# Inverse RMS roots at three of four places: ScalarE Sqrt, reciprocal and one Newton step in place of an integer seed and three Newton steps

## The reference

```python
def rmsnorm(x, g):
    xf = x.astype(jnp.float32)
    y = xf * lax.rsqrt(jnp.mean(xf * xf, axis=-1, keepdims=True) + EPS)
    return (y * g.astype(jnp.float32)).astype(x.dtype)
...
h = modulate(rmsnorm(x, norm_mix_g[l]), sh_m, sc_m)
z = jnp.einsum('bsd,de->bse', h, w_in[l])
...
y_a = spatial_gating(jax.nn.gelu(z_sgu), v_norm_g[l], sgu_w[l], sgu_b[l])
...
x = x + g_m[:, None, :] * jnp.einsum('bsd,de->bse', merged, w_out[l])
hf = modulate(rmsnorm(x, norm_ffn_g[l]), sh_f, sc_f)
x = x + g_f[:, None, :] * grouped_moe(hf, router_w, router_bias, ...)
return rmsnorm(x, final_norm_g)
```

## Time and profile before

| | us |
|---|---|
| median of 3 runs | 811.03 |
| lowest, highest | 810.52, 811.32 |
| span of the profiled execution | 808.6 |
| TensorE busy in it | 740.2 |
| VectorE busy in it | 600.2 |
| ScalarE busy in it | 383.4 |
| GpSimd busy in it | 196.5 |

### The profile page before, as it was taken

The page is one execution under the profiler, slowest core; times in us unless marked ns, Lnnn a source line. Parts: engine busy times, 40 slices in busy tenths (PEclk is TensorE's granted clock), DMA queues, the critical chain, the costliest instruction groups (busy, mean ns, idle before and its releaser), DMA issues. The chain is left out here.

```text
span 808.6 us, 10644 instructions
## 1 busy us (share of the span) xinstructions
PE 740.2 (92%) x3359; PEld 604.0 (75%) x3360; DVE 600.2 (74%) x823; ACT 383.4 (47%) x339; POOL 196.5 (24%) x74
## 2 busy tenths in 40 slices
PE   2589999999999999999999379999999999999982
PEld 2468888866888888887788368888888888888861
DVE  3772334766476666658556789999999999999976
ACT  5533523342323141324133266777777777777613
POOL 1000000400100000000052111445555554444552
PEclk9799999999999999999997589999999999999997
DMA  8797330431356473917472627599999999999652
GB/s 314 258 364 238 104 130 6 151 104 53 106 173 191 159 255 102 313 52 260 159 251 85 199 104 288 214 372 393 369 356 361 361 360 376 366 393 367 248 221 104
DMA packets 105075, 187.66 MB, mean 232 GB/s; under 512 B 6927, under 2 KB 49999, under 8 KB 104540
## 3 DMA queue, kind: packets, MB, share of 16 engines
q1 hardware_dynamic: 98652, 177.77, 61.8%
q0 software_dynamic: 4784, 7.95, 2.7%
q10 hardware_dynamic: 1616, 1.65, 0.6%
HBM read 180.47 MB, written 16.25 MB: 243 GB/s over the span
## 5 line engine op out<-in xcount | busy, mean ns | idle before, releaser
L747 DVE TENSOR_TENSOR wsplit<-raw,wsplit 128x2048 fp32r<-128x2048 f32 x132 | 299.3, 2288 | 78.9 <-ACT wsplit L521 53.8
L684 ACT ACTIVATE wsplit<-raw 128x2048 fp32r<-128x2048 f32 x96 | 183.9, 1918 | 74.3 <-PE ps L1323 74.3
L469 POOL DMA_INDIRECT expert_rows<-work,dest_now x15 | 108.1, 7209 | 114.3 <-DVE work L1227 114.3
L1321 PE MATMUL ps<-wsplit,hgT 128*128 128x512 f32 x272 | 110.1, 405 | 5.0 <-DVE hgT L1146 5.0
L1323 PE MATMUL ps<-wsplit,hgT 128*128 128x512 f32 x272 | 107.6, 395 | 0.0
L1322 PE MATMUL ps<-wsplit,hgT 128*128 128x512 f32 x272 | 106.8, 392 | 0.0
L1321 PE MATMUL ps<-hT,wsplit 128*128 128x512 f32 x256 | 102.5, 400 | 1.0 <-DVE mx L900 1.0
L1322 PE MATMUL ps<-hT,wsplit 128*128 128x512 f32 x256 | 101.1, 395 | 0.0
L1323 PE MATMUL ps<-hT,wsplit 128*128 128x512 f32 x256 | 101.1, 395 | 0.0
L799 DVE SCALAR_TENSOR_TENSOR raw<-raw,c_silu 128x256 f32 (+1 forms) x128 | 62.0, 484 | 17.1 <-DMA raw<-in_w_ada 13.1
L1321 PEld LDWEIGHTS ps<-wsplit,hgT 128*128 128x128 f32 x272 | 51.9, 191 | 15.6 <-DVE hgT L1146 5.7
(11 more groups left out here) (241 smaller groups left out, 1207.7 us busy)
## 6 DMA issues: line engine op xcount, KB each, us to landing
raw<-in_w_exp_gate SPq DMA_DIRECT2D x32, 1024.0 KB
raw<-in_w_exp_up SPq DMA_DIRECT2D x32, 1024.0 KB
raw<-in_w_exp_down SPq DMA_DIRECT2D x32, 1024.0 KB
raw<-in_w_ada SPq DMA_DIRECT2D x24, 1024.0 KB
raw<-in_w_in SPq DMA_DIRECT2D x20, 1024.0 KB
expert_rows<-tmp SPq DMA_DIRECT2D x4, 1024.0 KB, 12.4
raw<-in_w_branch_a SPq DMA_DIRECT2D x4, 1024.0 KB
raw<-in_w_branch_b SPq DMA_DIRECT2D x4, 1024.0 KB
```

The costliest lines, as they stand in the source:

```text
L469: g.indirect_dma_start(out=y_dram, out_offset=bass.IndirectOffsetOnAxis(ap=dest_now[:, 0:1], axis=0), in_=y, in_offset=None, bounds_check= ...
L684: A_(wsplit[:, c, 0, :], raw[:, c, :], ACT.Copy).then_inc(hi_ready, 1)
L747: V.tensor_tensor(wsplit[:, n, 1, :], raw[:, slot, :], wsplit[:, n, 0, :].bitcast(F32), ALU.subtract).then_inc(lo_ready, 1)
L1321: nc.tensor.matmul(out, w_hi, m_hi_, start=first, stop=False)
```

## The change

Three of the four inverse roots are computed in another way: those of the first norm, of the FFN norm and of the last norm. The one of the spatial gate (`inv_rms(20, NT)`) stays. ScalarE takes the square root of mean + EPS with its Sqrt function, from the sums in `stats`, right behind the squares; VectorE takes the reciprocal z, and makes one Newton step, z (1.5 - 0.5 m z z). For that EPS must lie in a tile (`eps_col`, one more memset on GpSimd), and the function table with Sqrt must be loaded on ScalarE. `root_table` does a Sqrt of one column ahead of each of the three places, so that the load stands there: behind the Silu at the start, behind the last high part of `merged`, and behind the last tile's hidden rows in the tail. Each brings one ACT_TABLE_LOAD that wasn't there. The loads for Gelu, Sigmoid, Exp and Silu stay as many as they were.

```diff
@@ gpsimd @@
             g.memset(base[:, :], 0.0)
+            g.memset(eps_col[:, :], EPS)
@@ scalar @@
+            def square_root(col, n):
+                A_(root[:, 0:n], stats[:, col:col + n], ACT.Sqrt, bias=eps_col[:, 0:1],
+                   scale=1.0 / D).then_inc(rooted, 1)
+
+            def root_table(use):
+
+                A_(root[:, NT + use:NT + use + 1], eps_col[:, :], ACT.Sqrt)
+
             act.wait_ge(cols_ready, 1)
             A_(c_silu[:, :], cols[:, 0:ND], ACT.Silu).then_inc(c_ready, 1)
+            act.wait_ge(consts, 1)
+            root_table(0)
...
+            act.wait_ge(squares, NT)
+            square_root(0, NT)
             act.wait_ge(rms_ready, 1)
...
                 A_(hT[:, 0, k, :], merged[:, k, :], ACT.Copy).then_inc(m_hi, 1)
+            root_table(1)
             for n in range(O0 + 1, O0 + 4):
...
                 A_(hf[:, t, :], x_tiles[:, t, :], ACT.Square, accum_out=stats[:, 24 + t:25 + t]).then_inc(sq2, 1)
+                act.wait_ge(sq2, t + 1)
+                A_(root[:, t:t + 1], stats[:, 24 + t:25 + t], ACT.Sqrt, bias=eps_col[:, 0:1],
+                   scale=1.0 / D).then_inc(rooted, 1)
...
             a_hi(tiles - 1)
 
+            root_table(2)
             act.wait_ge(y_ready, tiles - 1)
...
+            act.wait_ge(fin_sq, NT)
+            square_root(28, NT)
             act.wait_ge(fin_rms_ready, 1)
@@ vector @@
-            def inv_rms_1(col):
...
+            def root_inverse(col, n, count):
+
+                m, half, z = stats[:, col:col + n], nrm[:, 0:n], nrm[:, NT:NT + n]
+                step(V.tensor_scalar(half, m, -0.5 / D, -0.5 * EPS, ALU.mult, ALU.add))
+                dve.wait_ge(rooted, count)
+                step(V.reciprocal(z, root[:, 0:n]))
                 done()
+                step(V.tensor_tensor(m, z, z, ALU.mult))
                 done()
+                step(V.tensor_tensor(m, m, half, ALU.mult))
+                done()
+                step(V.scalar_tensor_tensor(out=m, in0=m, scalar=1.5, in1=z, op0=ALU.add, op1=ALU.mult))
+                done()
+
+            def root_inverse_1(t):
+
+
+                m, half, z, q = stats[:, 24 + t:25 + t], nrm[:, 0:1], nrm[:, NT:NT + 1], nrm[:, 2 * NT:2 * NT + 1]
+                step(V.tensor_scalar(half, m, -0.5 / D, -0.5 * EPS, ALU.mult, ALU.add))
+                dve.wait_ge(rooted, 2 + t)
+                step(V.reciprocal(z, root[:, t:t + 1]))
+                done()
+                step(V.scalar_tensor_tensor(out=q, in0=z, scalar=half, in1=z, op0=ALU.mult, op1=ALU.mult))
+                done()
+                step(V.scalar_tensor_tensor(out=m, in0=q, scalar=1.5, in1=z, op0=ALU.add, op1=ALU.mult))
+                done()
...
-            inv_rms(0, NT)
+            root_inverse(0, NT, 1)
...
-                inv_rms_1(24 + t)
+                root_inverse_1(t)
...
-            inv_rms(28, NT)
+            root_inverse(28, NT, NT + 2)
```

More of the change, by code:

```diff
@@ L91, in tokens_moe_kernel @@
         fin_rms = sb("fin_rms", [P, 1])
+        eps_col = sb("eps_col", [P, 1])
+        root = sb("root", [P, NT + 3])
         inv_count = sb("inv_count", [P, 16])
@@ L162, in tokens_moe_kernel @@
         h_aff, h_hi, h_lo = map(sem, ("h_aff", "h_hi", "h_lo"))
-        chain = sem("chain")
+        chain, rooted = sem("chain"), sem("rooted")
         v_gelu, v_centred, v_square, v_ready, u_ready = map(
@@ L772, in inv_rms @@
                     done()
-            def inv_rms_1(col):
[L777 to L782, removed]
+            def root_inverse(col, n, count):
[3 more added lines that the diff above has]
+                step(V.reciprocal(z, root[:, 0:n]))
                 done()
-                step(V.tensor_scalar(zi, powers[2].bitcast(I32), -0.5,
-                                     float(0x5F3759DF - (2 << 23) - (1 << 31)), ALU.mult, ALU.add))
+                step(V.tensor_tensor(m, z, z, ALU.mult))
                 done()
[L788 to L794, removed]
+                step(V.tensor_tensor(m, m, half, ALU.mult))
[12 more added lines that the diff above has]
+                done()
             def ada(acc, slot, a):
```

## The result

| | before | after |
|---|---|---|
| median, beside each other (us) | 811.17 (4 runs) | 802.27 (4 runs) |
| lowest, highest (us) | 810.52, 813.09 | 800.20, 803.69 |
| ratio | | 0.9887, 95% interval 0.9871 to 0.9902 |
| span of the profiled execution (us) | 808.6 | 801.9 |

The change gains 8.9 us, where 3.3 were forecast. The two profiled executions are 6.7 us apart and not 8.9, since they are the fastest of the four before and the slowest of the four after.

The account below looks back on a forecast made before the run. TensorE was taken to bound the body, and the chain through the norm the front and tail. Start 1.15, FFN norm 1.0 and tail 1.18 sum to 3.3 us off 811.0, giving 807.7; range 806.3 to 810.0.

Parts of the forecast that it names:

- Inside the body a faster VectorE is worth nothing beyond such a wait: In the TensorE-bound body, faster VectorE work gains only what TensorE spends waiting, 0.7 us on GpSimd's add in the FFN norm.
- Between 60 and 480 us it waits only around the router: Reading of TensorE's waits: only around the router, with 0.7 us on GpSimd and 0.2 us on ScalarE in the FFN norm.
- Start, 1.15 with bounds 0.8 and 1.25: First norm: from last read of the squares to first modulation operation 1.43 us in place of 2.58, a gain of 1.15.
- that wait as a sign of being wrong: At the start: the prediction is wrong if VectorE waits for w_ada at 13.6 us.
- FFN norm, 1.0 with ends 0.68 and 1.36: TensorE's 0.68 us wait for the third tile's hf goes; saves 1.36 if the clock's fall keeps its time; 1.0 taken.
- Everything behind hangs on this chain and shifts with it: Behind the FFN norm: router, gather and expert tiles all start earlier along with it.
- Tail, 1.18: Last norm: from last read of the squares to first scaling 1.53 us in place of 2.71, a gain of 1.18.
- Table loads: nothing: The three added table loads, at the start, before the out-projection's splits and in the tail, cost nothing, hidden by idle time.
- The rival by the Trainium skill: Each table load stalls ScalarE another 1.28 to 1.38 us, at start and tail; 808.3 to 809.2, take 808.8; chance 0.12.
- only the tail counts: Start's gain meets late w_ada or TensorE's restart, 0.68 becomes a wait for ScalarE; 1.2 us left, 809.8; chance 0.16.
- the clock takes it back: The clock's fall in the FFN norm comes sooner, costing up to 7.0 us, 814.7 with the whole price; chance 0.05.
- the third sign of being wrong: Whole kernel: the prediction is wrong if the stretches at 1.2 GHz are longer in sum.

Follow-up runs that it names:

- e1_pad64: The kernel before with one unused tile of 64 bytes in front of hT, nothing else changed; 807.02 us beside 812.54, ratio 0.993.
- e2_tiles_last: The changed kernel with its two new tiles declared behind `work`, so that hT keeps its old address; 810.66 us, ratio 0.9988.
- e11_both_pads: The kernel before with 64 unused bytes ahead of `raw` and 64 ahead of hT; 808.14 us in one run, beside 812.98.

## Why the prediction was wrong

- **What was missed.** The step is the sentence "Inside the body a faster VectorE is worth nothing beyond such a wait", and with it the assumption that TensorE's 740 us of work stay what they are. True of VectorE, but the sum then had no term for the body at all. The new tiles moved one operand of the wide matmuls by 64 bytes against the other, and that gave 5.5 us (e1_pad64). By stage it is 93.85 - 91.76 = 2.1, 2.75 and 1.2 us in A, B and C, together 6.1. None of the rivals held it, and no range built from the roots' terms could have. The evidence was at hand, though not its price: the kernel declares two new tiles ahead of hT, and its profile before has two means for what is the same matmul, 390 ns where both operands lie in wsplit and 395 to 400 where hT is streamed.
- **Direction.** That the kernel came out faster, clear of the noise, is owed to the 64 bytes, and is luck as far as the forecast goes: at the old addresses the roots gave 1.0 us with an interval that holds zero.
- **A reading.** "Between 60 and 480 us it waits only around the router" is not what the view says. It also has three waits of TensorE for VectorE, of 1.0, 1.0 and 0.9 us; the last, at the product with w_out, is where the start's gain went.
- **Start, 1.15 with bounds 0.8 and 1.25.** Right to its step: 0.30 for the root as taken, 1.63 in place of 2.58 gives 0.95, with a wait for w_ada of 0.31 us, where the bound left 0 to 0.3. The prediction had named that wait as a sign of being wrong; it cost 0.2 us against the forecast and is not what failed. What failed is that it was carried to the end. In e2_tiles_last 0.48 is left behind the restart near 61 us, and at w_out, where a transfer comes no earlier, nothing.
- **FFN norm, 1.0 with ends 0.68 and 1.36.** In e2_tiles_last 0.05 became 0.88 at the third tile and 1.14 behind the router, 1.1 in all; over all kernels 0.85. Right in cause and near in size, though the 0.68 us to be saved is one value of a wait that ran from nothing to 1.1 us in the kernels with the old root. "Everything behind hangs on this chain and shifts with it" failed: the gather gave back 0.85 of it, and the loop the rest.
- **Tail, 1.18.** 1.35 measured in after. The two handoffs around the root are 0.03 and 0.03 us, where 0.14 and 0.10 were taken for them: the root started at 792.48, 0.03 behind the read's end, and the reciprocal at 792.81 behind the root's end at 792.78.
- **Table loads: nothing.** Right. The rival by the Trainium skill, "ScalarE: Activation LUTs", What ACT_TABLE_LOAD costs, would have a further 1.38 us of drain at each load. The dummy roots start 0.02, 0.01 and 0.02 us behind the ends of the loads that start at 4.78, 376.66 and 770.63 us, and the loads themselves 0.02 us or less behind the activations ahead of them, so the measurement decides against it here.
- **Rival "only the tail counts", 1.2 us gained.** For the roots by themselves this came nearest: 1.3 us of span in e2_tiles_last, and 1.0 (-0.2 to 2.2) as time. Its reasons were others, a late w_ada or a restart; it was w_out and the gather. At the old addresses the interval holds the rival's 1.2 and neither the forecast's 3.3 nor its lower bound of 2.5. At the new ones the two estimates, 2.4 and 3.5 us, are too wide to decide between them.
- **Rival "the clock takes it back".** In part, and not because of the roots. The mean granted clock is 0.955 in after for 0.962 in before, the third sign of being wrong that the prediction gave; but it is 0.954 in e1_pad64, which has no new root. The fall in the FFN norm came 7.0 us behind the end of the wide matmuls before. In after it is in this stretch:

```profile
428.50:429.00 0.50, 0.50 (x6) 0.50 (x6) 0.50 (x1) 0.00 (x0) 0.00 (x0) 0.79 0.51 205
```

A mean of 0.79 puts the fall near 428.8, 5.6 us behind the transposes' start at 423.17, and the third tile's transposes then took 1.61 us for 1.10 in the earlier trace rows. That goes with an FFN stage 0.7 us shorter in after and not 1.1. But in the kernel with the new root at the start alone, which has the old FFN norm, it also fell early, 5.4 us behind, while in e2_tiles_last, with the new one, it was 6.9. The price there is 15.50 - 15.14 = 0.36 us between after and e2_tiles_last, and never the 7.0 of the rival. A second one stands in the tail: in after the clock is at one half from 783.8 to 787.2 us, and the last 20 wide matmuls take 6.42 us, behind a longer wait for ScalarE. Before and then after:

```profile
789.15 5.13 PE L1607 MATMUL ps<-wsplit,tail_sel 128*128 128x512 f32 x20 [2.65 <-ACT wsplit L717]
```

```profile
783.58 6.42 PE L1634 MATMUL ps<-wsplit,tail_sel 128*128 128x512 f32 x20 [3.64 <-ACT wsplit L737]
```

By these two, after's lead over before falls from 6.5 us at the end of the expert loop to 797.80 - 792.45 = 5.35 at the last read of the squares. The longer matmuls do not come from the roots: e11_both_pads, with no new root, has them (6.59), and e2_tiles_last, with all of them, has not (5.12). The wait is taken up in the last section.

## What to carry to other kernels

A change that declares or drops a tile moves everything that is placed behind it. Before a few microseconds are put down to new instructions, compare the time from one start to the next of the same wide matmuls in a stage that the change doesn't touch, and run the old kernel with an unused tile of the same size: it takes one line. Where TensorE is the bound, try the distance between streamed and held operand for itself; here one spare tile of 64 bytes was worth more than three rewritten normalizations. And a gain at the start counts only up to the first transfer whose landing doesn't move with it.

## What was not expected of the hardware

- Wide matmuls (128x512, fp32r) at 2.4 GHz took 227, 229 or 233 ns from start to start in the three long stages, by the distance of their two operands in on-chip memory modulo 256 bytes: 0, 64, and the others tried (32, 128, 192, 224). Shifting both together changed nothing. The first 70 or so, at a distance of 64, took 233.3 in one kernel and 229.1 in another with the same addresses.
- A GpSimd tensor_tensor on large tiles held up a VectorE operation of one element. Before, GpSimd and then VectorE:

```profile
408.32 9.41 POOL L477 TENSOR_TENSOR wsplit<-raw,wsplit 128x2048 fp32r<-128x2048 f32 x2 [202.99 <-ACT wsplit L521]
```

```profile
416.18 1.57 DVE L789 SCALAR_TENSOR_TENSOR nrm<-nrm 128x1 f32<-128x1 f32 x1
417.78 0.16 DVE L792 SCALAR_TENSOR_TENSOR nrm<-nrm 128x1 f32<-128x1 f32 x1
417.98 0.22 DVE L789 SCALAR_TENSOR_TENSOR nrm<-nrm 128x1 f32<-128x1 f32 x1
```

The same operation takes 0.22 us two rows on, and this one ends at 417.75, as GpSimd's work does (408.32 + 9.41 = 417.73). In after it is 1.52 us at the same place, up to 411.74 beside GpSimd's end at 402.34 + 9.38 = 411.72. It cost nothing, as TensorE was still in the product with w_out; but a short chain on VectorE is not short beside such work. In the tail, on the path itself, it does seem to cost. Two adds of VectorE on 128x1024 (L1285 before, L1312 in after) took 5.78 us in before and 6.71 in after, both times beside GpSimd's own adds on 128x1024. In e1_pad64, where GpSimd's last add waited for a DMA and started only as VectorE's first one ended, they took 3.57. TensorE's wait behind them was 2.7, 3.6 and 0.5 us. No experiment moved this work, so the cause is not shown; but 6.71 - 3.57 = 3.1 us is more than the last norm's new root saved.
